# Two attention layers of three: the split-precision scores in one pass of 128 rows and one of 64 instead of three of 128

## What is computed

```python
s_loc = jnp.einsum('bqhgd,bkhd->bhgqk', qs, ks).astype(jnp.float32) * scale
s_loc = jnp.where(valid, s_loc, NEG_INF)
s_ctx = jnp.einsum('bqhgd,bkhd->bhgqk', qs, kc).astype(jnp.float32) * scale
p = jax.nn.softmax(jnp.concatenate([s_loc, s_ctx, sink], axis=-1), axis=-1).astype(dt)
```

## Time and profile before

| | |
|---|---|
| median of 3 runs | 1317.66 us (1316.57 to 1320.43) |
| the profiled execution | 1317.76 us |
| its span in the trace | 1316.0 us |
| TensorE, matmuls | 1206.9 us, 92% of the span, 7724 instructions |
| TensorE, weight loads | 970.4 us, 74% |
| VectorE, ScalarE, GpSimd | 61%, 49%, 30% |

### The profile page before, as it was taken

One profiled execution on the slowest core, in us unless ns is written; L12 is line 12 of the kernel. 1 busy time (PEld: TensorE's weight loads), 2 busy tenths in 40 slices (PEclk: granted clock), 3 DMA queues, 4 the chain that ended last, 5 costly groups with the idle time before them and its releaser, 6 DMA issues.

```text
span 1316.0 us, 20311 instructions
## 1 busy us (share of the span) xinstructions
PE 1206.9 (92%) x7724; PEld 970.4 (74%) x7724; DVE 796.5 (61%) x1489; ACT 650.9 (49%) x1300; POOL 399.8 (30%) x218
## 2 busy tenths in 40 slices
PE   6699999999999899998999999998999899989784
PEld 2378888788887688886787777987778677767453
DVE  2442666666667426454787786467654666887834
ACT  3512455445446527633776677463444535454332
POOL 1533121212212625562000022275131245443432
PEclk9799999999999899999999999999999999999788
DMA  8441202221122511232202211302104024113001
GB/s 335 159 177 32 80 34 97 97 81 41 73 97 78 198 65 38 91 112 50 73 25 82 73 41 33 131 32 76 50 29 139 17 70 156 59 50 132 33 1 64
DMA packets 32508, 108.59 MB, mean 83 GB/s; under 512 B 3908, under 2 KB 4548, under 8 KB 32028
## 3 DMA queue, kind: packets, MB, share of 16 engines
q1 hardware_dynamic: 32412, 107.29, 23.9%
HBM read 102.44 MB, written 2.15 MB: 79 GB/s over the span
## 4 chain that ended last, share of the span: by engine, by line
PE 70%; DVE 15%; ACT 6%; issue 3%; DMA 3%; POOL 2%; SPq 0%; DVEq 0%; ACTq 0%
PE PS L575 29%; PE PS L558 16%; PE PS L681 8%; PE PS L669 7%; DVE AD L2013 3%; DMA AF<-wstream 2%; PE PS L609 2%; DVE AF L2045 2%; PE PS L872 2%; ACT AF L1110 1%; PE PS L776 1%; POOL AR L2110 1%; PE PS L598 1%; POOL AR L2124 1%; DVE AF L1540 1%
## 5 line engine op out<-in xcount | busy, mean ns | idle before, releaser
L575 PE MATMUL PS<-AR 128*128 128x512 f32 (+1 forms) x2424 | 505.2, 367 | 9.8 <-POOL AR L2110 4.7
L575 PEld LDWEIGHTS PS<-AR 128*128 128x128 f32 x2424 | 410.5, 191 | 91.0 <-issue 20.3
L2110 POOL TENSOR_TENSOR AR<-AF,AR 128x1024 fp32r<-128x1024 f32 x98 | 238.6, 2440 | 427.7 <-ACT AR L973 427.7
L558 PE MATMUL PS<-AR 128*128 128x256 f32 (+4 forms) x1556 | 295.2, 332 | 18.4 <-issue 8.5
L558 PEld LDWEIGHTS PS<-AR 128*128 128x128 f32 (+1 forms) x1556 | 228.3, 192 | 53.8 <-issue 26.0
L1680 DVE TENSOR_REDUCE AF<-PS 128x1 f32<-128x512 f32 (+3 forms) x192 | 145.3, 757 | 165.2 <-PE PS L558 160.4
L1110 ACT ACTIVATE AF<-PS 128x512 f32<-128x512 f32 (+3 forms) x192 | 124.4, 648 | 95.9 <-PE PS L669 90.8
L1101 ACT ACTIVATE AF<-PS,AF 128x512 f32<-128x512 f32 (+3 forms) x192 | 140.7, 733 | 22.2 <-DVE AF L1682 21.5
L669 PE MATMUL PS<-AF 128*128 128x128 f32 x864 | 128.8, 276 | 14.6 <-ACT AF L1110 12.1
L1697 DVE TENSOR_SCALAR AF<-AF 128x512 f32<-128x512 f32 (+3 forms) x192 | 126.0, 656 | 6.7
L669 PEld LDWEIGHTS PS<-AF 128*128 128x128 f32 x864 | 98.8, 141 | 41.2 <-issue 27.6
(11 more groups left out here) (185 smaller groups left out, 1180.9 us busy)
## 6 DMA issues: line engine op xcount, KB each, us to landing
AF<-wstream SPq DMA_DIRECT2D x170, 512.0 KB, 4.8
AD<-rows SPq DMA_DIRECT2D x4, 1024.0 KB, 9.4
AF<-rpb_band SPq DMA_DIRECT2D x16, 224.0 KB, 4.1
AF<-x_in SPq DMA_DIRECT2D x2, 1024.0 KB, 9.3
out<-AF SPq DMA_DIRECT2D x8, 256.0 KB, 2.4
AF<-rope SPq DMA_DIRECT2D x2, 512.0 KB, 4.5
AF<-ctx_in SPq DMA_DIRECT2D x1, 1024.0 KB, 6.3
AR<-AR SPq DMA_DIRECT2D x16, 64.0 KB, 2.5
```

The source lines that it names most:

```text
L558: mm = pe.matmul(out, stationary, moving, start=i == 0, stop=i == len(products) - 1)
L575: mm = pe.matmul(out[:, 0:t1 - t0], a, b, start=k == 0 and i == 0, stop=k == nk - 1 and i == 2)
L2110: pool.tensor_tensor(w[:, 1, :], RAW[:, c % N_RAW, :], w[:, 0, :].bitcast(F32), ALU.subtract).then_inc(lo_done, 1)
```

## The change

In layers 1 and 3 the three products of a score segment become two. Per head the stationary tile now has that head's high query rows on its own 64 rows, and its low query rows on the other 64. The keys' high part is held twice, on both halves, so one matmul over 128 rows gives high by high plus low by high. A second matmul over only the head's own 64 rows multiplies the high queries by the low keys. No zeros are needed, so both clearings and their waits go. To fill the tiles: `split_keys` makes one more rounded copy per half, `high_q` is two copies of 64 rows instead of one of 128, `low_q` two subtractions of 64 rows that cross to the other half, each with a wait of GpSimd on its own semaphore behind it (and two waits ahead of them), `evac_c` issues two instructions for the queries and four for the keys, and `low_c` two for the queries. `q_lo` counts two per pair.

```diff
--- before.py
+++ after.py
-        KZ = tiles(R2, 2, 2, 2, T)
+        ROWS_OF = [slice(0, 64), slice(64, 128)]
+        KA, KAL = tiles(R2, 2, 2, T), tiles(R2[:, 4 * T:], 2, T)
...
-        KC = tiles(R2[:, 2048:], 2, 2, 2, S)
+        KC, KCL = tiles(R2[:, 2048:], 2, 2, S), tiles(R2[:, 4096:], 2, S)
...
-        kz_zero, kc_zero = sem("keys_zeroed_a"), sem("keys_zeroed_c")
...
@@ -462,17 +462,18 @@
...
                     for half in range(2):
                         near = [b for b in (t - 1, t, t + 1) if 0 <= b < QT] if part == "x" else []
-                        segments = []
+                        segments, own = [], ROWS_OF[half]
                         if near:
                             c0 = 512 - P * len(near)
                             m0 = 0 if t > 0 else P
                             k0 = near[0] * P
-                            segments.append((c0, P * len(near), [(identR, mask3R[:, m0:m0 + P * len(near)])] + [
-                                (QA[:, a, p % 2, q0:q0 + P], KZ[:, b, tile, half, k0:k0 + P * len(near)])
-                                for a, b in ((0, 0), (0, 1), (1, 0))]))
+                            segments.append((c0, P * len(near), [
+                                (identR, mask3R[:, m0:m0 + P * len(near)]),
+                                (QA[:, p % 2, half, q0:q0 + P], KA[:, tile, half, k0:k0 + P * len(near)]),
+                                (QA[own, p % 2, half, q0:q0 + P], KAL[own, tile, k0:k0 + P * len(near)])]))
                         segments.append((512, C, [
-                            (QA[:, a, p % 2, q0:q0 + P], KZ[:, b, tile, half, S:T])
-                            for a, b in ((0, 0), (0, 1), (1, 0))]))
+                            (QA[:, p % 2, half, q0:q0 + P], KA[:, tile, half, S:T]),
+                            (QA[own, p % 2, half, q0:q0 + P], KAL[own, tile, S:T])]))
...
@@ -497,11 +498,11 @@
         for p in range(N_NA):
             for t in range(QT):
                 for half in range(2):
-                    q = [QC[:, a, p % 2, t * P:t * P + P] for a in range(2)]
+                    q, own = QC[:, p % 2, half, t * P:t * P + P], ROWS_OF[half]
                     d0 = (6 - 2 * t) * GRID
                     unit(c0=0, c1=S, segments=[
                         (0, S, [(identR, BIAS[p % 2][a][:, half, d0:d0 + S]) for a in range(2)]
-                         + [(q[a], KC[:, b, p % 2, half, :]) for a, b in ((0, 0), (0, 1), (1, 0))])],
+                         + [(q, KC[:, p % 2, half, :]), (q[own], KCL[own, p % 2, :])])],
...
@@ -779,7 +780,7 @@
...
             def ready_a(p):
-                pe.wait_ge(q_lo, p + 1)
+                pe.wait_ge(q_lo, 2 * p + 2)
...
@@ -1074,7 +1075,7 @@
                 elif what[0:2] == "qg":
                     p = int(what[2:])
                     if p >= 1:
-                        act.wait_ge(q_lo, p)
+                        act.wait_ge(q_lo, 2 * p)
...
@@ -1333,11 +1334,14 @@
                 if what in "qk" and p >= 2:
                     act.wait_ge(s_ready, pair_scored("C", p - 2))
                 if what == "q":
-                    act.activation(QC[:, 0, p % 2, :], acc, ACT.Identity, bias=col("bna", p)).then_inc(c_hi, 1)
+                    for half, h in enumerate(ROWS_OF):
+                        ins = act.activation(QC[h, p % 2, half, :], acc[h, :], ACT.Identity, bias=col("bna", p)[h, :])
+                    ins.then_inc(c_hi, 1)
                 elif what == "k":
-                    for half in range(2):
-                        h = slice(64 * half, 64 * half + 64)
-                        ins = act.activation(KC[h, 0, p % 2, half, :], acc[h, :], ACT.Identity, bias=col("bna", 4 + p)[h, :])
+                    for half, h in enumerate(ROWS_OF):
+                        for rows in ROWS_OF:
+                            ins = act.activation(KC[rows, p % 2, half, :], acc[h, :], ACT.Identity,
+                                                 bias=col("bna", 4 + p)[h, :])
                     ins.then_inc(c_hi, 1)
...
@@ -1349,7 +1353,6 @@
...
             bias_high(0)
-            act.wait_ge(kc_zero, 1)
...
@@ -1634,24 +1637,24 @@
             def split_keys(j):
 
                 wait_read(f"A.k{j}.c")
-                dve.wait_ge(kz_zero, 1)
-                for half in range(2):
-                    h = slice(64 * half, 64 * half + 64)
-                    step(dve.tensor_copy(KZ[h, 0, j, half, :], QP[h, :]))
-                    low = dve.tensor_tensor(KZ[h, 1, j, half, :], QP[h, :], KZ[h, 0, j, half, :].bitcast(F32), ALU.subtract)
+                for half, h in enumerate(ROWS_OF):
+                    step(dve.tensor_copy(KA[h, j, half, :], QP[h, :]))
+                    dve.tensor_copy(KA[ROWS_OF[1 - half], j, half, :], QP[h, :])
+                    low = dve.tensor_tensor(KAL[h, j, :], QP[h, :], KA[h, j, half, :].bitcast(F32), ALU.subtract)
                     if half == 1:
                         signal(low, kz_done, j + 1)
 
             def rope_q(p):
                 if p >= 1:
-                    dve.wait_ge(q_lo, p)
+                    dve.wait_ge(q_lo, 2 * p)
                 rope_turned(f"A.q{p}.rot", QP[:, 0:S], QP[:, 0:S])
 
             def high_q(p):
                 dve.wait_ge(tanh_done, 2 * p + 1)
                 if p >= 2:
                     dve.wait_ge(s_ready, pair_scored("A", p - 2))
-                signal(dve.tensor_copy(QA[:, 0, p % 2, :], QP), q_hi, p + 1)
+                dve.tensor_copy(QA[ROWS_OF[0], p % 2, 0, :], QP[ROWS_OF[0], :])
+                signal(dve.tensor_copy(QA[ROWS_OF[1], p % 2, 1, :], QP[ROWS_OF[1], :]), q_hi, p + 1)
...
 
@@ -1941,13 +1944,13 @@
                 dve.wait_ge(c_hi, lows_c[0])
                 acc = wait_acc(name)
                 if what == "q":
-                    ins = dve.scalar_tensor_tensor(QC[:, 1, p % 2, :], acc, col("bna", p),
-                                                   QC[:, 0, p % 2, :].bitcast(F32), ALU.add, ALU.subtract)
+                    for half, h in enumerate(ROWS_OF):
+                        ins = dve.scalar_tensor_tensor(QC[ROWS_OF[1 - half], p % 2, half, :], acc[h, :], col("bna", p)[h, :],
+                                                       QC[h, p % 2, half, :].bitcast(F32), ALU.add, ALU.subtract)
                 else:
-                    for half in range(2):
-                        h = slice(64 * half, 64 * half + 64)
-                        ins = dve.scalar_tensor_tensor(KC[h, 1, p % 2, half, :], acc[h, :], col("bna", 4 + p)[h, :],
-                                                       KC[h, 0, p % 2, half, :].bitcast(F32), ALU.add, ALU.subtract)
+                    for half, h in enumerate(ROWS_OF):
+                        ins = dve.scalar_tensor_tensor(KCL[h, p % 2, :], acc[h, :], col("bna", 4 + p)[h, :],
+                                                       KC[h, p % 2, half, :].bitcast(F32), ALU.add, ALU.subtract)
...
@@ -1962,7 +1965,6 @@
...
                 step(dve.scalar_tensor_tensor(XL[:, k, :], XL[:, k, :], col("fg", k), RSTD2[:, 0, :], ALU.mult, ALU.mult))
-            dve.wait_ge(kc_zero, 1)
...
@@ -2138,9 +2140,13 @@
                 if p >= 2:
                     pool.wait_ge(s_ready, pair_scored("A", p - 2))
                 pool.wait_ge(q_hi, p + 1)
-                pool.tensor_tensor(QA[:, 1, p % 2, :], QP, QA[:, 0, p % 2, :].bitcast(F32), ALU.subtract).then_inc(q_lo, 1)
-
-            pool.memset(R2.bitcast(F32), 0.0).then_inc(kz_zero, 1)
+                pool.wait_ge(cos_done, ropes[0])
+                pool.wait_ge(lo_done, fed[0])
+                for half, h in enumerate(ROWS_OF):
+                    pool.tensor_tensor(QA[ROWS_OF[1 - half], p % 2, half, :], QP[h, :],
+                                       QA[h, p % 2, half, :].bitcast(F32), ALU.subtract).then_inc(q_lo, 1)
+                    pool.wait_ge(q_lo, 2 * p + half + 1)
+
...
             need("C.v2", 1)
-            b, i = tasks["B.o5.0"]
-            pool.wait_ge(acc_ready[b], i)
-            pool.memset(R2[:, 2048:].bitcast(F32), 0.0).then_inc(kc_zero, 1)
...
```

## The result

The change makes the kernel slower. After: 1357.86 us, median of 4 runs (1353.55 to 1360.48), against 1317.9 us for the kernel before on the same chip; ratio 1.030, 95% interval 1.027 to 1.033. The forecast was 1355 us. The profiled execution took 1357.24 us (span 1355.4 us, granted clock 0.966), that of before 1317.76 us (0.969). The gap between the two is 39.5 us.

What follows compares the result with a forecast made beforehand. TensorE was taken to bound both changed attention stages. Exposed switches less removed matmuls 35.7 us, ScalarE in layer 3 1.9 and GpSimd in layer 1 0.3 add 37.9 to 1317.76: 1355.7, given as 1355 us; range 1325 to 1366.

Steps and rivals of the forecast that it cites:

- The price of a change of shape: TensorE, each switch between 128-row and 64-row passes: 0.20 us between fp32r matmuls, 0.16 us into transposes; 384 switches.
- Rival B: TensorE: entry or exit of a 64-row pass alone drains, 0.10 us per switch on average; 1325 us; chance 0.07.
- What waits hide, in layer 1: Layer 1, TensorE's 24 waits (10.8 us) before its second turn: they hide 3.8 us of context units, 3.0 at t = 3.
- nearly gone: Sign expected in layer 1's trace: the 24 waits before TensorE's second turn, 10.8 us together, almost disappear.
- The start of layer 1: Start of layer 1's attention: GpSimd's halves at 1.85 us each delay low_q and the weight split behind it, +0.3 us.
- The key step of layer 3: Layer 3, four ScalarE key instructions instead of two: TensorE's second turn waits some 0.6 us, three pairs, +1.9 us.
- Layer 3, the rest: Layer 3's 32 units cost +0.13 us each; the 8 in steps where TensorE waits cost nothing, 1.0 us hidden.
- Rival C: The clock falls too: half-clock score stretches, one in each of layer 1's 8 pairs, 2 in layer 3; 1365 us; chance 0.08.
- Rival A: TensorE: no drain, 64-row passes stream like any other, 28.3 us saved less 5.7 in waits; 1297 us; chance 0.10.
- The clearings: Both clearings went unseen in the kernel before, so removing them gains 0.

Runs made afterwards that it cites:

- grouped: The changed kernel with the two 64-row passes of each layer 1 x unit one behind the other, same instructions; 1331.01 us, ratio 1.012.
- padded variant: The changed kernel with low keys held per half, zeros in the other 64 rows, second pass over 128 rows, clearings back; 1313.24 us, ratio 0.998.
- the two experiments: The padded variant (1313.24 us), and the kernel before with its third product left out in layers 1 and 3 (1308.77 us, ratio 0.995).

## Why the prediction was right

**The price of a change of shape.** Taken as 0.20 us between fp32r matmuls and 0.16 into transposes, from a column shape and from 4 rows. Units came out at +0.50, +0.43 and +0.22 for +0.52, +0.47 and +0.24, and grouped gives 0.18 for a change. So 64 rows are a shape of their own. Rival B, half a switch, falls with it. The rule of the Trainium skill that I cited ("TensorEngine Tiling (Array Packing)", Key Properties: changing the tiling mode drains TensorE) fits here for 64 rows, at 0.18 to 0.20 us for a change; between 96 and 128 rows the runs show no such price. That the array runs empty meanwhile is the Trainium skill's reading and mine; the runs show the price alone.

**What waits hide, in layer 1.** Of the 24 waits of the second turn, 16 are left with 6.6 us, as the waits of after show; "nearly gone" was too much: 6.8 us hidden in 10.8 leave 4.0 by my own sum.

```profile
PEld PS L559 <- issue: 27.3, 102, 0.9
...
PEld PS L670 <- issue: 6.6, 16, 0.5
```

Layer 1 cost 30.8 us; predicted were 32.6 (39.4 for its x and context units, less 6.8 hidden) and 0.3 for its start, so 2.1 us too many.

**The start of layer 1.** L2146 stands in the chain twice. TensorE starts at 121.29 (121.37 before), with the stage 0.3 us ahead of before: some 0.2 us later, for 0.3 predicted. Halves take as long as the whole, which was the value I took.

```profile
117.33 1.83 POOL AR L2146
...
119.24 1.81 POOL AR L2146
...
121.29 2.98 PE PS L559 x10
```

**The key step of layer 3.** Predicted was a wait of some 0.6 us for 3 pairs, 1.9 us. The timeline of after, first of the three:

```profile
961.62 2.77 ACT L1343 ACTIVATE AR<-PS,AF 64x512 fp32r<-64x512 f32 x4 [4.10 <-PE PS L576]
...
964.42 0.60 ACT L1111 ACTIVATE AF<-PS 128x512 f32<-128x512 f32 x1
...
965.16 0.63 PE L670 MATMUL PS<-AF 128*128 128x128 f32 x4 [0.76 <-ACT AF L1111]
```

The wait is 0.76 us here, but the term was mis-sized: the second turn comes 3.54 us after ScalarE starts on the keys (965.16 - 961.62), and before it was 2.54 (932.61 - 930.07). So a pair pays 1.0 us, not 0.6. My own numbers gave 0.82 (933.43 - 932.61), and I took 0.26 off for the longer scores, which don't shift the turn when ScalarE's copy ends last; the other 0.18 is mostly the 0.14 us from the end of that copy to the turn. The other two key steps show the same 3.54 us, so the term is 3.0 us, not 1.9.

**Layer 3, the rest.** 11.0 us measured, 5.1 predicted (4.2 for its units, less 1.0 hidden, and 1.9). The missing term is the clock. No run has after's code in layer 3 at before's clock, so its size is an estimate. By the traces' records of the granted clock (0.96, 0.92 and 0.98 of full speed over the stage), before spent 10.1 us of it at half clock, after 23.0 and grouped 6.3. Between the last two that is 16.7 us for a difference of 7.3 us, 0.44 us each. At before's clock after would then have lost 11.0 - 0.44 x 12.9 = 5.3 us, and some 5.7 us are clock. The 5.3 agree with the 5.1 in sum only: the key step took 3.0 of them for 1.9, and the units some 2.3 for 3.2.

Rival C had it with 2 such stretches in layer 3 and 8 in layer 1. In layer 1 after shows just one, in the first projection (6.99 us for the 24 matmuls at 124.27, 5.67 later on); in layer 3 they came more than in before, and more than C's 2 (23.0 us against 10.1). The same four score matmuls in after, at half clock and at full:

```profile
979.63 1.71 PE PS L559 x4
...
993.00 1.11 PE PS L559 x4
```

**What was luck.** The profiled executions are 39.5 us apart for 37.9 predicted, but its parts did not come out that well. Layer 1 was 2.1 us too high in the sum and layer 3 5.9 us too low, and after gained 2.4 us outside both, which no term had.

**Rival A was mis-sized, and this could have cost the sign.** It gave 1297 us if changes of shape are free. The padded variant is that case, and it took 1313 us. I hid the removed time only in the 24 waits that stood in the trace, 5.7 us. In fact the removed matmuls lengthen them and open others (38 and 44 such waits in the two experiments). Had 64 rows been free, the result would have been "the same", not 1.6% faster. Behind TensorE at 97% busy stood a softmax chain barely shorter than it. The clearings came back in the padded variant, at half their size, and nothing waited for them, as predicted: behind the second (1.81 us) GpSimd still waited 3.05 us for ScalarE.

## What to carry to other kernels

Count changes of the array's shape before counting matmuls: at 0.18 to 0.20 us each, two of them cost more than a 256-wide matmul (0.12 us) saves. Where a smaller contraction is needed between full ones, pad it with zeros or keep it at 96 rows; passes put next to each other lose less (1331 us against 1358) but still lose. And when time is taken from an engine that is 97% busy, look at what its work covers: run the kernel with that work left out before building the change, since that bounds the gain (here 6.7 us of 28.3).

## What the runs showed of the hardware that I had not expected

- 96 rows cost no more than 128 in the stream: ratio 0.998 with 192 changes between the two, and 0.998 with none. 64 rows cost 0.18 to 0.20 us for each change.
- GpSimd's subtraction over 64 rows by 768 takes 1829 ns, over 128 rows 1824 ns; its copy of 64 by 512 took 0.64 us.
- One and the same kernel spread over 10.9 us (1315.47 to 1326.41) with its granted clock (0.972 to 0.963), and the same layer 3 code took 136.52 us in one kernel (clock 0.98) and 143.86 in another (0.92). A stage's few microseconds are to be compared only with the clock of that stage beside them.
